# The second block's RMS norms: sums on four column groups, modulated tiles in SBUF

## The reference, cut to what matters

```python
def rms_norm(x, g):
    ms = jnp.mean(jnp.square(x), axis=-1, keepdims=True)
    return x * lax.rsqrt(ms + RMS_EPS) * g
...
h = rms_norm(x, norm1_g) * (1 + scale) + shift
h = h @ w_in
...
x = x + gate * (merged @ w_out)
h = rms_norm(x, norm2_g) * (1 + scale2) + shift2
x = x + gate2 * conv_ffn(h)
```

## Time and profile before

| | us |
|---|---|
| runs of the kernel before | 2907.47, 2907.35, 2895.26 |
| their median | 2907.35 |
| the profiled execution's own time | 2900.13 |
| its span | 2898.3 |
| TensorE busy (share of the span) | 2814.4 (97%) |
| VectorE, ScalarE, GpSimd busy | 1141.3 (39%), 1424.6 (49%), 1965.9 (68%) |
| mean granted clock of TensorE | 0.978 |

### The profile page before, as it was taken

The page is one execution under the profiler, slowest core; times in us unless marked ns, Lnnn a source line. Parts: engine busy times, 40 slices in busy tenths (PEclk is TensorE's granted clock), DMA queues, the critical chain, the costliest instruction groups (busy, mean ns, idle before and its releaser), DMA issues.

```text
span 2898.3 us, 51897 instructions
## 1 busy us (share of the span) xinstructions
PE 2814.4 (97%) x21902; PEld 2620.1 (90%) x21902; DVE 1141.3 (39%) x2066; ACT 1424.6 (49%) x1943; POOL 1965.9 (68%) x816
## 2 busy tenths in 40 slices
PE   7999989999999899999999999999999998999999
PEld 7889979998889799988899998778999987889999
DVE  2432331123223222333644344546524365663434
ACT  4656444446565434445554445445644444565443
POOL 6556738866557358867676886765667877657687
PEclk9999999999999899999999999999999999999999
DMA  7445455564456445564444554543445554434453
GB/s 252 174 173 202 151 193 181 184 217 171 173 184 213 151 168 183 182 214 168 140 159 152 176 184 151 193 145 117 139 153 182 176 199 153 138 125 168 146 181 132
DMA packets 136520, 495.78 MB, mean 171 GB/s; under 512 B 15072, under 2 KB 17376, under 8 KB 135136
## 3 DMA queue, kind: packets, MB, share of 16 engines
q1 hardware_dynamic: 131904, 480.53, 48.6%
q10 hardware_dynamic: 4384, 11.93, 1.2%
HBM read 489.26 MB, written 3.15 MB: 170 GB/s over the span
## 4 chain that ended last, share of the span: by engine, by line
PE 88%; DVE 5%; ACT 2%; DVEq 2%; issue 1%; ACTq 1%; DMA 1%; POOL 0%; SPq 0%
PE lin L519 17%; PE lin L520 17%; PE lin L521 17%; PE aux L519 5%; PE aux L521 5%; PE aux L520 5%; PE lin L545 3%; PE lin L547 3%; PE lin L546 3%; PE aux L614 2%; PE aux L692 1%; PE aux L947 1%; DVE Z L1515 1%; PE aux L714 1%; PE aux L660 1%
## 5 line engine op out<-in xcount | busy, mean ns | idle before, releaser
L495 POOL TENSOR_TENSOR wlo<-raw,whi 128x1024 fp32r<-128x1024 f32 x812 | 1965.7, 2437 | 923.0 <-ACT whi L1055 922.5
L1055 ACT ACTIVATE whi<-raw 128x1024 fp32r<-128x1024 f32 x812 | 849.2, 1057 | 734.3 <-PE lin L521 489.3
L519 PE MATMUL lin<-in_hi,whi 128*128 128x256 f32 x3520 | 1019.4, 290 | 26.3 <-POOL wlo L495 22.0
L520 PE MATMUL lin<-in_lo,whi 128*128 128x256 f32 x3520 | 1001.8, 285 | 0.0
L521 PE MATMUL lin<-in_hi,wlo 128*128 128x256 f32 x3520 | 1001.8, 285 | 0.0
L519 PEld LDWEIGHTS lin<-in_hi,whi 128*128 128x128 f32 x3520 | 681.6, 194 | 63.9 <-issue 50.6
L520 PEld LDWEIGHTS lin<-in_lo,whi 128*128 128x128 f32 x3520 | 681.7, 194 | 0.5
L521 PEld LDWEIGHTS lin<-in_hi,wlo 128*128 128x128 f32 x3520 | 680.9, 193 | 0.0
L519 PE MATMUL aux<-br_hi,whi 128*128 128x256 f32 x880 | 249.1, 283 | 0.0
L520 PE MATMUL aux<-br_lo,whi 128*128 128x256 f32 x880 | 249.0, 283 | 0.0
L521 PE MATMUL aux<-br_hi,wlo 128*128 128x256 f32 x880 | 249.0, 283 | 0.0
(11 more groups left out here) (251 smaller groups left out, 3731.6 us busy)
## 6 DMA issues: line engine op xcount, KB each, us to landing
raw<-in_wstream SPq DMA_DIRECT2D x908, 512.0 KB, 3.3
Z<-in_rel ACTq DMA_DIRECT2D x2, 1536.0 KB, 8.9
Z<-in_mem_t ACTq DMA_DIRECT2D x2, 1024.0 KB, 7.0
kv_store<-Z ACTq DMA_DIRECT2D x2, 1024.0 KB, 6.8
Z<-kv_store ACTq DMA_DIRECT2D x2, 1024.0 KB, 14.7
x<-in_x_t SPq DMA_DIRECT2D x1, 1024.0 KB, 5.1
Z<-in_ctx_t SPq DMA_DIRECT2D x1, 1024.0 KB, 4.8
out_x<-x SPq DMA_DIRECT2D x1, 1024.0 KB, 3.9
```

What stands on the lines that cost most here:

```text
L495: pool.tensor_tensor(wlo[s][:, :], raw[i % RAWS][:, :], whi[s][:, :].bitcast(F32), ALU.subtract).then_inc(lo_pool, 1)
L519: pe.matmul(out, wh, xh, start=start, stop=False, skip_group_check=True)
L520: pe.matmul(out, wh, xl, start=False, stop=False, skip_group_check=True)
L1055: act.activation(whi[s % SLOTS][:, :], raw[i % RAWS][:, :], ACT.Copy).then_inc(hi_ready, 1)
```

## The change

TensorE's sums: seven of the eight squared tiles are summed by products with 32 columns of ones, tile k into rows 32 (k mod 4) of a 128 x 256 result in PSUM (`shares`), where each row of a group holds the same sum. It waits for squares in five parts instead of four (two, two, two, one and one tile). VectorE copies `shares` to SBUF (`copy_shares`); two products with a column of 1/32 add the four groups to the sums of the last tile, which is summed as before. Eleven empty products stand in four places: two, one and three within the sums and ahead of the spread, and five behind it.

VectorE's modulation: per tile one instruction (L1987) multiplies the tile, the scale and the spread values into an SBUF tile; ScalarE writes `in_hi` as that tile plus the shift (L1356), and VectorE writes `in_lo` as (tile + shift) - `in_hi` (L1992). The first chunk waits for its inputs tile by tile (`fresh=TILES`). The residual signals per tile.

ScalarE's order: the table load for Sqrt moves from the start of the norm to the mixer's end ahead of seven `hi_part` calls, and to the FFN's end ahead of the last `hi_part` calls, at all three FFNs. The `hi_part` between the squares moves behind the fourth `in_hi`; the next function's table is loaded behind the eighth.

```diff
+PARTS = (0, 1), (2, 3), (4, 5), (6,), (7,)
...
+        shares, share_copy = aux[:, 0, T:2 * T], probs[:, 0:T]
...
             def rms():
-                token_sums(MG, 0)
+                for tiles in PARTS[:-1]:
+                    pe.wait_ge(sq_ready, t.next(sq_ready))
+                    for k in tiles:
+                        rows = slice(32 * (k % 4), 32 * (k % 4) + 32)
+                        mm = pe.matmul(shares[rows, :], ones[:, 0:32], zt(MG + k), start=(k < 4), stop=(k >= 3), skip_group_check=True)
+                mm.then_inc(shares_done, 1)
+                keep_busy(2, 2)
+                pe.wait_ge(sq_ready, t.next(sq_ready))
+                for tt in range(2):
+                    pe.matmul(square_sums(1)[:, tt:tt + 1], zt(MG + 7)[:, tt * P:(tt + 1) * P], ones[:, 0:1],
+                              start=(tt == 0), stop=False, skip_group_check=True)
+                keep_busy(1, 2)
+                pe.wait_ge(shares_ready, t.next(shares_ready))
+                for tt in range(2):
+                    mm = pe.matmul(square_sums(1)[:, tt:tt + 1], share_copy[:, tt * P:(tt + 1) * P], share[:, :],
+                                   start=False, stop=True, skip_group_check=True)
+                mm.then_inc(var_ready, 1)
+                keep_busy(3, 2)
                 spread_inverse(0)
-                keep_busy(10)
+                keep_busy(5)
...
                 hidden(NCH - 1, 4)
+                if conv:
+                    act.preload_act_table(ACT.Sqrt)
                 for q in range(4):
                     if context_norm:
                         quarter_hi(q, ctx_scaled[:, quarter(q)])
                     hi_part()
...
+            def modulated_hi(shift, k):
+                act.wait_ge(x_ready, t.next(x_ready))
+                act.activation(in_hi[:, k * T:(k + 1) * T], scaled_tile(k), ACT.Identity, bias=mod[:, shift + k:shift + k + 1]).then_inc(x_hi, 1)
+
+            def rms(x, shift, then=None):
+                for tiles in PARTS:
+                    act.wait_ge(resid2, t.next(resid2, len(tiles)))
+                    s = slice(tiles[0] * T, (tiles[-1] + 1) * T)
+                    act.activation(zt(MG + tiles[0], len(tiles)), x[:, s], ACT.Square).then_inc(sq_ready, 1)
+                norm_root(1, 1)
+                for k in range(KD):
+                    modulated_hi(shift, k)
+                    if k == 3:
+                        hi_part()
                 if then:
                     act.preload_act_table(then)
...
-            for q in range(3):
-                hi_part()
-                quarter_hi(q, scaled(q))
+            for k in range(6):
+                if k % 2 == 0:
+                    hi_part()
+                modulated_hi(0, k)
             evacuate(1, 1, zt(VL + 4, 4))
-            quarter_hi(3, scaled(3))
+            modulated_hi(0, 6)
+            modulated_hi(0, 7)
...
             def rms_modulate(x, i, shift):
                 inverse_std()
                 dve.wait_ge(inverse_wide, t.next(inverse_wide))
+                for k in range(KD + 1):
+                    if k < KD:
+                        dve.scalar_tensor_tensor(scaled_tile(k), x[:, k * T:(k + 1) * T], mscale[:, 8 * i + k:8 * i + k + 1], inverse_out(0),
+                                                 ALU.mult, ALU.mult).then_inc(x_ready, 1)
+                    if k:
+                        o = slice((k - 1) * T, k * T)
+                        dve.wait_ge(x_hi, t.next(x_hi))
+                        dve.scalar_tensor_tensor(in_lo[:, o], scaled_tile(k - 1), mod[:, shift + k - 1:shift + k], in_hi[:, o].bitcast(F32),
+                                                 ALU.add, ALU.subtract).then_inc(inputs_ready, 1)
+                settle()
+
+            def copy_shares():
+                dve.wait_ge(shares_done, t.next(shares_done))
+                copy(share_copy, shares).then_inc(shares_ready, 1)
```

More of the change, by code:

```diff
@@ L52 @@
 LATB = 11
-HALVES, QUARTERS = (0, 4), (0, 2, 4, 6)
+HALVES, QUARTERS, TILES = (0, 4), (0, 2, 4, 6), tuple(range(8))
+PARTS = (0, 1), (2, 3), (4, 5), (6,), (7,)
 Q2, K2, VL, VC, YB, MG, GB, S2 = 0, 8, 24, 32, 40, 48, 56, 64
@@ L289, in build @@
         sq_ready = sem("sq_ready")
+        shares_done = sem("shares_done")
+        shares_ready = sem("shares_ready")
         var_ready = sem("var_ready")
@@ L464, in scaled, with scaled_tile @@
             return aux[:, 2 + q % 2, :]
+        def scaled_tile(k):
+            return zt(MG + k)
         block = ctx.enter_context(nc.Block())
@@ L527, in feature_units @@
                 for k0 in range(0, kn, kper):
-                    if k0 in fresh:
-                        pe.wait_ge(inputs_ready, t.next(inputs_ready))
                     wh, wl = next_unit()
                     for k in range(k0, k0 + kper):
+                        if k in fresh:
+                            pe.wait_ge(inputs_ready, t.next(inputs_ready))
                         for j, (c, w) in enumerate(tiles):
@@ L623, in spread_inverse, with ffn @@
                 mm.then_inc(inverse_wide, 1)
-            def ffn(after=(), context_norm=False):
+            def ffn(after=(), context_norm=False, fresh=QUARTERS):
                 def down(hp):
@@ L634, in down @@
                         mm.then_inc(units_used, 1)
-                feature_chunk(0, fresh=QUARTERS, after=after)
+                feature_chunk(0, fresh=fresh, after=after)
                 if context_norm:
@@ L1017, in second_layer @@
                 rms()
-                ffn()
+                ffn(fresh=TILES)
             pe.sem_inc(units_used, SLOTS)
@@ L1452, in second_layer @@
                 input_hi(in_hi[:, half(1)], lin[:, 0, :])
+                act.preload_act_table(ACT.Sqrt)
                 hi_parts(7)
-                rms(x, True, ACT.Silu)
+                rms(x, 24, ACT.Silu)
                 ffn(True)
@@ L1968, in gated_residual @@
                             dve.scalar_tensor_tensor(xs, aux[:, k // 2, (k % 2) * T:(k % 2 + 1) * T], mod[:, gate + k:gate + k + 1], xs,
-                                                     ALU.mult, ALU.add)
-                        settle().then_inc(resid2, 1)
+                                                     ALU.mult, ALU.add).then_inc(resid2, 1)
+                settle()
             def maps(ap, tt):
@@ L2210, in second_layer @@
                 gated_residual(x, 16)
+                copy_shares()
                 rms_modulate(x, 1, 24)
```

27 lines of the change are left out of this document (9 added, 18 removed).

## The result

The changed kernel takes 2887.29 us (median of 9 runs, 2879.96 to 2892.32); the kernel before takes 2901.27 us in 9 runs on the same chip. The ratio is 0.995 with an interval of 0.9938 to 0.9963: 14.0 us faster, between 11 and 18. The prediction was 2885, with 18.0 us of gain.

What follows compares the result with a forecast made beforehand. TensorE, busy 97% of the span, was taken as the bound, with useless or half-clock work at the norms. -25.9 + 0.4 + 3.5 + 3.3 + 0.7 gave -18.0 us: 2882 from the profiled execution, stated as 2885, range 2870 to 2902.

Steps and rivals of the forecast that it cites:

- The stretches: At the five norms, last residual pair to next chunk's first product: 56.58 us shrinks, gaps summing to 25.9 us gained.
- G: Start of the last residual pair on VectorE at a norm; the forecast's times in the stretch count from it.
- Rival 3: Column groups of the norms' sums run one after another: some 2 us a norm, 10 in all, 2895 us; chance 0.06.
- The 0.23 us for a change between column modes: In each norm's sums, TensorE idle time per mode switch, taken from L660 and added once per norm.
- The clock: New chain at the norms priced at full clock, with the spread at half of its 1.22 us.
- Rival 1: Clock still falls to half in the norms' new gaps: 11 to 16 us given back, about 2898 us; chance 0.14.
- The FFN ends: Table load ahead of the high part TensorE needs next: about 1.1 us lost at each of three ends, 3.3 us.
- The latent norm: Nearly every `in_lo` waits for GpSimd, delaying the next weight, all of it on TensorE: cost 3.5 us (0 to 5).
- The port at the norms: One of a norm's last four `in_lo` waits up to 2.4 us for GpSimd; nothing taken, 0.4 for the fourth norm.
- Rival 2: Several GpSimd splits during a norm's `in_lo` delay each: 8 us a norm, 40 in all, 2925 to 2930; chance 0.07.
- where I had put 0.7: Allowance in the sum for stretches at half clock that remain: 0.7 us given back.

Runs made afterwards that it cites:

- one-edit run: Changed kernel with only the Sqrt table load at the FFN ends moved behind the last four high parts; 2882.13 us, ratio 0.994 to the kernel before.
- the combined one: Changed kernel plus FFN-end table load behind high parts, latent norm through PSUM, small loads before stores, two empties for three before the spread; 2877.80 and 2881.25 us.

## Why the prediction came out as it did

- **The stretches.** Predicted 5.8, 6.2, 5.8, 7.1, 5.8; measured 6.05, 6.47, 6.05, 7.29, 6.05. The gain was 25.9 by the sum and is 23.5 by the rows: the sum started from 56.58, which is 1.2 too much (see the result), and the new stretches are 0.2 to 0.3 longer than forecast, all of it behind the spread. The pieces that were off: `in_hi` from an SBUF tile with a bias takes 0.51 us (the nearest form had 0.38), `in_lo` 0.48 (0.42), the product of tile 6 0.62 (0.35, from G + 1.0 to G + 1.35); the pairs of one-column products 0.34 on the chain (0.49). Rival 3, groups one after another, is out: twelve records on column groups, six tiles, take 0.99 us. The 0.23 us for a change between column modes, taken from another place of the kernel, doesn't show: on the chain of the result the rows follow each other with at most 0.04 us between them.
- **The clock.** Taken at 1.00, and it is. Rival 1 was wrong for this kernel and names the mechanism that the run without empties shows. That the fall is paid in the next chunk was in its price. That the sums on column groups bring mainly the clock was in the sum only through the spread and the empties at full clock, and not put as plainly as the runs put it.
- **The FFN ends.** 3.3 predicted; 3.7 measured as waits, and the one-edit run took 4.3 off, both by the medians and by the length of the three FFNs. Right in place and mechanism, and 1 us small.
- **The latent norm.** 3.5 predicted. The wait is there, 2.36 us, but the step "all of it on TensorE" failed: the next wait, for VectorE ahead of the spatial product, shrank from 3.65 to 1.68. Net 0.4. I had followed the delay to the next unit and not to the next wait behind it. Nor did nearly every `in_lo` wait: four of the eight took 1.4 to 2.3 us, the others 0.47 to 0.48. By its length the way to the spatial product grew by 1.4 to 2.9 us in the three profiles, more than the waits: 2.2 us of clock are missing on it before, 3.4 to 5.1 there. In the run with the table load behind, with the same code at this place, it is 86.1 us with 1.7 missing, so whether the delay brings the clock down is open.
- **The port at the norms.** One `in_lo` per norm waits for GpSimd and costs nothing, as forecast. The line's durations (min/median/max) in the changed kernel:

```profile
L1992 DVE SCALAR_TENSOR_TENSOR in_lo<-Z,mod,in_hi x48: 472/481/2332, 1561.8 to 2699.7; 128x256 fp32r<-128x256 f32 x48
```

  Rival 2 needed more than one such wait per norm. The rule of the Trainium skill ("SBUF — State Buffer", section "Who interferes with whom") is borne out: `in_lo` takes 0.47 us alone, and at the first norm the slow one runs from 1565.35 to 1567.68 us, beside a GpSimd split of 2.40 us that ends at 1567.39.
- **What was not foreseen.** In the latent's layer 1 VectorE's normalisation ahead of the spatial product, two SBUF to SBUF instructions, met GpSimd splitting eleven units in a row; before, it fell mostly into a pause of GpSimd. VectorE before, then VectorE and GpSimd in the changed kernel:

```profile
2395.30 1.00 DVE L2148 TENSOR_SCALAR Z<-Z,small 128x512 f32<-128x512 f32 x2
2384.60 4.62 DVE L2185 TENSOR_SCALAR Z<-Z,small 128x512 f32<-128x512 f32 x2
2365.16 26.27 POOL L504 TENSOR_TENSOR wlo<-raw,whi 128x1024 fp32r<-128x1024 f32 x11 [4.46 <-ACT whi L1081]
```

  The two instructions took 1.00 us together before and 4.62 here, and TensorE waited 2.28. From the fourth norm's first product to that spatial product pass 33.58 us in place of 30.68, 2.9 more. With the old sums or the old modulation it is 32.6 and 33.0, so neither main part alone brings it. That it is the port is read from the rows; a version with that step on another engine was not tried.
- **The remainder.** In lengths, the norms gave 23.5 us, the FFNs took 4.3, the latent norm's waits 0.4 and the latent's layer 1 2.9: -23.5 + 4.3 + 0.4 + 2.9 = -15.9, against -14.0 by the medians, whose interval goes from 11 to 18. The rest is the clock outside the norms, profile by profile: (1 - clock) over the span, norms left out, is 45.9 us in the profile of before and 54.5, 47.6 and 50.2 in three of the changed kernel, which is 8.6, 1.7 and 4.3 more. Added to -15.9 that gives -7.3, -14.2 and -11.6, and these spans are 7.8, 14.9 and 11.6 us shorter than that of before. Part of this differs from run to run of one kernel, part looks regular: from 1410 us to some 30 us ahead of the end it is 11.9 us before and 17.0 in each of the three profiles, 5.1 us more, where I had put 0.7. In the kernel with the table load behind and in the combined one it is 13.6. Why the clock falls oftener there, beside the new waits or by how the waits fall in time, is not settled; before has one profile only.
- **How near it came.** 18.0 us were forecast and 14.0 measured, and part of this nearness is luck. The latent norm was put 3.1 us too high by its waits, which stood against 2.9 us in the latent's layer 1 that were not in the sum. What is left is the 2.4 us that the norms fell short, 1 us at the FFN ends, and the clock outside the norms.

## What to carry to other kernels

Where TensorE idles or feeds single columns between two products, price the stretch twice: its own length, and the clock in it and behind it; sums that stream many columns, with a few empty products among them, were worth as much here as the shorter modulation on VectorE and ScalarE. A table load goes where the engine waits for TensorE anyway, not ahead of the piece that TensorE needs next. Follow a new wait to the one behind it before counting it, and try loads that somebody waits for ahead of stores on the same queue: here their issues fell from 4.1 us to 1.3 in all.

## What the runs showed of the hardware

- Time follows the granted clock. In the 14 runs of the kernel before in the last group the mean clock goes from 0.974 to 0.981 and the time from 2908.3 to 2892.5 us; in the first nine of the changed kernel from 0.981 to 0.986 and from 2892.3 to 2880.0, that is 23 and 25 us for each 0.01. The spread of 12 to 16 us between runs of one kernel goes with this. Up to 1410 us, ahead of all that the change touches, (1 - clock) sums to between 28.9 and 35.7 us in three profiles of the changed kernel.
- A fall of the clock can come behind an idle stretch, when TensorE is busy again: in the run without empties TensorE was idle from 1555 to 1556 us at full clock, and fully busy when the clock fell 0.5 us later.
- The issues of the three small loads on ScalarE take 0.34 to 0.46 us ahead of the two stores of 1 MB and 1.16 to 1.74 behind them (1.24 to 1.39 in the kernel before).
